# A transformer stack's third feed-forward stage in three packed pairs of steps, with keys and values packed ahead of them

## What is computed

```python
def swiglu(x, w_gu, w_down):
    gate, up = jnp.split(x @ w_gu, 2, axis=-1)
    return (jax.nn.silu(gate) * up) @ w_down

    # first block, layer 0
    x = x + 0.5 * swiglu(rms_norm(x, ffn1_norm[0]), ffn1_w_gu[0], ffn1_w_down[0])      # ffn0
    # gated delta rule and memory attention                                            # ain, mem, out0
    x = x + 0.5 * swiglu(rms_norm(x, ffn2_norm[0]), ffn2_w_gu[0], ffn2_w_down[0])      # ffn1
    ckr = rms_norm(x, kv_in_norm) @ w_dkv
    c_kv = rms_norm(ckr[..., :KV_LORA], kv_lat_norm)
    k_rope = apply_rope(ckr[..., None, KV_LORA:], cos, sin)[:, :, 0]
    k_nope, v_mla = jnp.split((c_kv @ w_ukv).reshape(b, s, B_HEADS, QK_NOPE + V_HEAD), [QK_NOPE], axis=-1)
    # layer 1
    x = x + 0.5 * swiglu(rms_norm(x, ffn1_norm[1]), ffn1_w_gu[1], ffn1_w_down[1])      # ffn2
    # latent attention and memory attention                                            # bin, uq, out1
    x = x + 0.5 * swiglu(rms_norm(x, ffn2_norm[1]), ffn2_w_gu[1], ffn2_w_down[1])      # ffn3
    # second block: pooling, convolutions, differential attention                      # in2, out2
    x = x + (silu(h2 @ w_gate) * (h2 @ w_up)) @ w_down                                 # ffn4
```

## Time and profile before

| | |
|---|---|
| median of three runs | 1291.8 us |
| the profiled execution | 1291.59 us |
| its span | 1289.4 us |
| TensorE (matmuls) busy | 1274.9 us, 99% |
| VectorE busy | 950.1 us, 74% |
| ScalarE busy | 819.0 us, 64% |
| 16 DMA engines moved | 313 MB, 243 GB/s |

### The profile page before, as it was taken

One profiled execution on the slowest core, in us unless ns is written; L12 is line 12 of the kernel. 1 busy time (PEld: TensorE's weight loads), 2 busy tenths in 40 slices (PEclk: granted clock), 3 DMA queues, 4 the chain that ended last, 5 costly groups with the idle time before them and its releaser, 6 DMA issues.

```text
span 1289.4 us, 17186 instructions
## 1 busy us (share of the span) xinstructions
PE 1274.9 (99%) x6940; PEld 1064.7 (83%) x6940; DVE 950.1 (74%) x1105; ACT 819.0 (64%) x1064; POOL 57.2 (4%) x85
## 2 busy tenths in 40 slices
PE   7999999999999999999999999999999999999998
PEld 6888888889988888888787888888888898788887
DVE  5788777778567888776353557678887798688885
ACT  7666658766566666674443466566666857766663
POOL 0000000000000000000000000000000100000000
PEclk9999999999999999999999999999999999999999
DMA  8987748887156677799787766876778874657772
GB/s 338 317 311 226 245 158 287 271 262 228 56 204 249 217 274 263 229 318 312 242 288 249 250 193 189 247 299 228 261 261 258 282 247 154 252 201 259 266 248 70
DMA packets 46686, 313.02 MB, mean 243 GB/s; under 512 B 5196, under 2 KB 7500, under 8 KB 9872
## 3 DMA queue, kind: packets, MB, share of 16 engines
q1 hardware_dynamic: 34080, 227.74, 46.5%
q0 software_dynamic: 11376, 81.54, 25.2%
q10 hardware_dynamic: 1152, 2.66, 0.6%
HBM read 310.85 MB, written 52.44 MB: 282 GB/s over the span
## 4 chain that ended last, share of the span: by engine, by line
PE 94%; DVE 2%; ACT 1%; DMA 1%; issue 0%; SPq 0%; DVEq 0%; ACTq 0%
PE ps L2847 24%; PE ps L2848 24%; PE ps L2849 24%; PE ps L2762 8%; PE ps L2998 2%; PE ps L2773 1%; PE ps L2880 1%; PE ps L2888 1%; PE ps L2893 1%; PE ps L549 1%; PE ps L551 1%; PE ps L550 1%; DVE w_lo_part L1732 1%; DMA arena<-in_tiles 1%; PE ps L2903 1%; PE ps L2820 1%
## 5 line engine op out<-in xcount | busy, mean ns | idle before, releaser
L1732 DVE TENSOR_TENSOR w_lo_part<-w_raw,w_hi_part 128x2048 fp32r<-128x2048 f32 (+2 forms) x184 | 416.2, 2267 | 120.3 <-ACT w_hi_part L674 120.1
L674 ACT ACTIVATE w_hi_part<-w_raw 128x2048 fp32r<-128x2048 f32 (+1 forms) x183 | 346.4, 1896 | 137.3 <-PE ps L2849 129.5
L2847 PE MATMUL ps<-w_hi_part,x_hi 128*128 128x512 f32 (+1 forms) x740 | 289.7, 391 | 0.8 <-DVE w_lo_part L1732 0.5
L2849 PE MATMUL ps<-w_hi_part,x_lo 128*128 128x512 f32 (+1 forms) x740 | 282.4, 382 | 0.0
L2848 PE MATMUL ps<-w_lo_part,x_hi 128*128 128x512 f32 (+1 forms) x740 | 281.4, 380 | 0.0
L2847 PE MATMUL ps<-w_hi_part,h_hi_part 128*128 128x512 f32 x464 | 186.0, 401 | 0.0
L2848 PE MATMUL ps<-w_lo_part,h_hi_part 128*128 128x512 f32 x464 | 181.2, 391 | 0.0
L2849 PE MATMUL ps<-w_hi_part,h_lo_part 128*128 128x512 f32 x464 | 181.2, 391 | 0.0
L674 ACT ACTIVATE w_hi_part<-arena 128x2048 fp32r<-128x2048 f32 x66 | 125.8, 1916 | 68.8 <-DMA arena<-in_tiles 35.9
L1732 DVE TENSOR_TENSOR w_lo_part<-arena,w_hi_part 128x2048 fp32r<-128x2048 f32 x66 | 150.2, 2288 | 24.3 <-ACT w_hi_part L674 23.9
L2849 PEld LDWEIGHTS ps<-w_hi_part,x_lo 128*128 128x128 f32 x740 | 139.1, 188 | 27.5
(11 more groups left out here) (462 smaller groups left out, 1553.4 us busy)
## 6 DMA issues: line engine op xcount, KB each, us to landing
w_raw<-in_tiles SPq DMA_DIRECT2D x179, 1024.0 KB, 6.7
made_sums<-in_tiles POOLq DMA_DIRECT2D x48, 1024.0 KB, 8.3
arena<-made_sums SPq DMA_DIRECT2D x24, 1024.0 KB, 7.8
arena<-in_tiles POOLq DMA_DIRECT2D x18, 1024.0 KB, 11.0
arena<-in_tiles SPq DMA_DIRECT2D x9, 1024.0 KB, 8.5
mem_kv<-in_tiles POOLq DMA_DIRECT2D x6, 1024.0 KB, 10.9
w_raw<-in_tiles SPq DMA_DIRECT2D x3, 512.0 KB, 6.4
arena<-in_w_ukv POOLq DMA_DIRECT2D x1, 1536.0 KB, 14.4
```

Of the source, the lines that this page charges most:

```text
L674: nc.scalar.activation(WH[:, n % RING, 0:w], source(n), ACT.Copy).then_inc(S["w_hi"], 1)
L1732: nc.vector.tensor_tensor(WL[:, n % RING, 0:w], source(n), WH[:, n % RING, 0:w], ALU.subtract).then_inc(S["w_split"], 1)
L2847: nc.tensor.matmul(o, a_hi, w_hi, start=start, stop=False, skip_group_check=True)
L2849: return nc.tensor.matmul(o, a_lo, w_hi, start=False, stop=stop, skip_group_check=True)
```

## The change

ffn2 becomes a stage of packed pairs too, three of them (steps 5, 7, 9). Its steps 0 to 4 stay plain, and all pieces of keys and values stand among them (`late_steps` on TensorE, `from_five` on ScalarE and VectorE). The blocks of x that the sums start from are copied out of PSUM by VectorE there (`x_blocks`), not by ScalarE. Some areas move: the sums' source, one hidden block and the three snapshots of ffn2 lie at the arena's end, the latent and the compressed keys lie further up, the padded rotary keys in the first memory keys' place.

GpSimd's queue makes 30 sums ahead in place of 24, and in another order: three for ffn2 before ffn1, three in ffn2; those for ffn3 from ffn2's third down tile to out1, those for ffn4 one in ffn3 and seven in in2 and out2. SyncE waits for each sum (`made_sum`) and no longer for all of a stage. The load of the two weights of keys and values is issued somewhat sooner. `plain_order`, the plain `ffn` of each engine and the tables of the orders are gone; functions of the stage's name give the orders.

The diff, cut to its core:

```diff
+
+    return (5, 7, 9) if name == "ffn2" else (3, 5, 7, 9)
...
-def quad_order():
-
-    order = [("g0", 0), ("g1", 0), ("g0", 1), ("g1", 1), ("d", 0), ("g0", 2), ("g1", 2)]
-    for s in QUAD_STEPS:
+def quad_order(name):
+
+    first = steps_of(name)[0]
+    order = [("g0", 0), ("g1", 0)]
+    for s in range(1, first):
+        order += [("g0", s), ("g1", s)] + ([("d", s - 1)] if s < first - 1 else [])
+    for s in steps_of(name):
         order += [("p5", s), ("m2", s), ("m1", s), ("p3", s), ("m6", s), ("d", s - 2), ("m7", s), ("d", s - 1), ("m4", s)]
     return order + [("d", 10), ("d", 9)]
...
             def t_load(name, s, k):
 
-                dst, (sem, _) = ((TA[QUAD_STEPS.index(s) % 2], t1_loaded(name, s)), (TC, t3_loaded(name, s)))[k]
+                dst, (sem, _) = ((ta_of(name, s), t1_loaded(name, s)), (TC, t3_loaded(name, s)))[k]
+                sp.wait_ge(*made_sum(name, s, k))
                 sp.dma_start(dst, made[quad_no(name, s), k, :, :]).then_inc(sem, 16)
...
+                if n == unit_of["ffn2", "g1", 4]:
+                    sp.wait_ge(S["kv_ps"], 6)
+                    t_load("ffn2", 5, 0)
+                if n == unit_of["ffn2", "d", 3]:
+                    sp.wait_ge(S["kv_ps"], 11)
+                    t_load("ffn2", 5, 1)
+                    t_load("ffn2", 7, 0)
                 for name in QUADS:
-                    if n == unit_of[name, "g1", 1]:
-                        sp.wait_ge(*made_all(name))
+                    if name != "ffn2" and n == unit_of[name, "g1", 1]:
                         sp.wait_ge(S["x_ready"], 4 * (X_OF[name] - 1) + 1)
-                        t_load(name, QUAD_STEPS[0], 0)
-                    if n == unit_of[name, "d", 0]:
+                        t_load(name, 3, 0)
+                    if name != "ffn2" and n == unit_of[name, "d", 0]:
...
+                def x_blocks(half):
+
+                    for k in range(4):
+                        last = nc.vector.tensor_scalar(blocks[:, 2 * half:2 * half + 2, k, :], PS[:, half:4:2, k * P:(k + 1) * P],
+                                                       gain(name, 4 * half + k), None, ALU.mult)
+                    if half:
+                        last.then_inc(S["x_blocks"], 1)
+
...
+                def from_five():
+
+                    for u in range(4):
+                        turned_hi(name, u)
+                    w_hi(at("g0", 1))
+                    first()
+                    w_hi(at("g1", 1))
+                    gate(0, 0)
+                    gate(0, 1)
+                    act.wait_ge(S["x_blocks"], 2 * of_all(name) + 1)
+                    kv_turned(0)
+                    kv_turned(1)
+                    w_hi(at("d", 0))
+                    hidden_hi(0)
+                    kv_turned(2)
+                    kv_turned(3)
+                    w_hi(at("g0", 2))
+                    gate(1, 0)
+                    gate(1, 1)
+                    w_hi(at("g1", 2))
+                    kv_down(0)
+                    w_hi(at("d", 1))
+                    hidden_hi(1)
+                    kv_down(1)
+                    kv_deviation()
+                    w_hi(at("g0", 3))
+                    sines()
+                    kv_rope()
+                    s_hi()
+                    gate(2, 0)
+                    gate(2, 1)
+                    w_hi(at("g1", 3))
+                    w_hi(at("d", 2))
+                    hidden_hi(2)
...
+                def from_five():
+
+                    start()
+                    w_lo(at("g0", 1))
+                    first()
+                    x_blocks(0)
+                    x_blocks(1)
+                    plain_hidden(0, 0)
+                    plain_hidden(0, 1)
+                    w_lo(at("g1", 1))
+                    hidden_lo(0)
+                    w_lo(at("d", 0))
+                    angles()
+                    w_lo(at("g0", 2))
+                    plain_hidden(1, 0)
+                    plain_hidden(1, 1)
+                    s_sums()
+                    w_lo(at("g1", 2))
+                    lambdas()
+                    w_lo(at("d", 1))
+                    hidden_lo(1)
+                    kv_scaled()
+                    w_lo(at("g0", 3))
+                    plain_hidden(2, 0)
+                    plain_hidden(2, 1)
+                    kv_rope()
+                    w_lo(at("g1", 3))
...
+                    pe.wait_ge(S["x_blocks"], 2 * of_all(name) + 1)
+                    down_half(0, 0)
+                    kv_down(0)
+                    down_half(0, 1)
+                    turn_pair(1)
+                    kv_down(1)
+                    quad_gate_up(2, 0)
+                    kv_turn_rope()
+                    quad_gate_up(2, 1)
+                    kv_swap()
+                    down_half(1, 0)
+                    down_half(1, 1)
+                    turn_pair(2)
+                    kv_turn_latent()
+                    quad_gate_up(3, 0)
+                    kv_keys(0)
+                    quad_gate_up(3, 1)
+                    kv_keys(1)
+                    down_half(2, 0)
+                    kv_keys(2)
+                    down_half(2, 1)
+                    turn_pair(3)
+                    kv_values(0)
+                    quad_gate_up(4, 0, lambda: kv_values(1))
+                    kv_values(2)
+                    quad_gate_up(4, 1)
+                    pe.wait_ge(S["kv_sb"], 14)
+                    for s in steps:
+                        quad_of_steps(s)
+                    down_half(10, 0)
+                    turn_pair(9)
+                    down_half(10, 1)
...
+            def t4_sum(name, s):
+
+                split(name, "m6", s)
+                pool.dma_start(ta_of(name, s), stored(name, "g1", s), accum_op=ALU.add).then_inc(t4_added(name, s)[0], 16)
+
+            def make(name, i):
+
+                copy(name, i)
+                add(name, i)
 
             for s in PAIR_STEPS:
                 pair_sums("ffn0", s)
             paced(tile0["ain"])
             makes("ffn1", 0, [tile0["ain"] + 2 * t + 1 for t in range(6)] + [tile0["mem"], tile0["mem"] + 1])
-            t4_sums("ffn1")
-            pool.wait_ge(S["tile_used"], unit_of["ffn1", "m4", QUAD_STEPS[-1]] + 1)
+            paced(tile0["mem"] + 2)
+            makes("ffn2", 0, [tile0["mem"] + 3])
+            make("ffn2", 1)
+            make("ffn2", 2)
+            for s in steps_of("ffn1"):
+                t4_sum("ffn1", s)
+            pool.wait_ge(S["tile_used"], unit_of["ffn1", "m7", 9] + 1)
             pool.dma_start(KVD, d["w_dkv"].rearrange("p (a b) -> p a b", b=2 * P + ROPE)).then_inc(S["side_loaded"], 16)
+            split("ffn1", "m4", 9)
             pool.dma_start(KVU, d["w_ukv"].rearrange("p (a b) -> p a b", b=2 * BH * P)).then_inc(S["side_loaded"], 16)
-            paced(tile0["ffn2"] + 1)
-            makes("ffn3", 0, range(tile0["ffn2"] + 4, tile0["ffn2"] + 28, 3))
-            paced(tile0["ffn2"] + 27)
-            makes("ffn4", 0, [tile0["ffn2"] + 30])
-            pool.wait_ge(S["kv_ps"], 11)
+            split("ffn2", "g0", 1)
+            makes("ffn2", 3, [unit_of["ffn2", "d", 0], unit_of["ffn2", "g1", 2], unit_of["ffn2", "g0", 3]])
+            makes("ffn3", 0, [unit_of["ffn2", "d", 2], unit_of["ffn2", "g1", 4]])
+            for s in steps_of("ffn2"):
+                t4_sum("ffn2", s)
+            copy("ffn3", 2)
+            split("ffn2", "m4", 9)
             pool.dma_start(RELB[:, :], d["rel_bias"]).then_inc(S["side_loaded"], 16)
             pool.dma_start(TABLE, d["rel_table"]).then_inc(S["side_loaded"], 16)
-            makes("ffn4", 1, [tile0["uq"], tile0["out1"]])
+            add("ffn3", 2)
+            makes("ffn3", 3, [tile0["bin"], tile0["uq"], tile0["uq"] + 1])
             pool.wait_ge(S["bias_row"], 1)
 
             pool.dma_start(bass.AP(bias_line, 0, [[2 * SEQ, MH], [1, 2 * SEQ]]), BROW).then_inc(S["bias_dma"], 16)
             pool.wait_ge(S["bias_dma"], 16)
-            makes("ffn4", 3, [tile0["out1"] + 1, tile0["out1"] + 2])
-            t4_sums("ffn3")
+            makes("ffn3", 6, [tile0["out1"], tile0["out1"] + 1])
+            for s in steps_of("ffn3"):
+                t4_sum("ffn3", s)
+            make("ffn4", 0)
...
+            makes("ffn4", 1, [tile0["in2"] + 2, tile0["in2"] + 4, tile0["in2"] + 6, tile0["in2"] + 8])
+            make("ffn4", 5)
+            make("ffn4", 6)
+            make("ffn4", 7)
+            for s in steps_of("ffn4"):
+                t4_sum("ffn4", s)
```

638 lines of the change are left out of this document (277 added, 361 removed).

## The result

The changed kernel took 1295.9 us (median of 7 runs, 1294.4 to 1298.0), beside it the kernel before 1291.8 us (7 runs, 1290.4 to 1293.6). The ratio is 1.0033, with an interval of 1.0023 to 1.0042: **slower, by 4.1 us** (0.3%, and clear of the noise), where 6.9 us faster was forecast. The profiled execution took 1295.2 us (span 1293.4).

What follows compares the result with a forecast made beforehand. TensorE, busy 99% of the span, was taken to bound the kernel. Terms of -6.9 + 0.2 = -6.7 us on the profiled 1291.6 us gave 1284.9 us, range 1283.4 to 1288.0 us.

Steps and rivals of the forecast that it cites:

- Products: Third feed-forward stage: three packed pairs take out 36 matmuls of 512 columns, 2.31 us a pair, 6.9 us saved.
- Joints: Third stage, tight handovers to TensorE around the moved keys and values: 0.2 us lost for all together.
- (a): VectorE makes eight blocks of x before the second g1 tile's split: 0 us, 1.9 us late at its bound.
- (b): The swap needs ScalarE's rope copy: 1.0 us to spare, so 0 us; 0.5 us late at its bound.
- (c): The latent's turn needs the rotated keys: 0.4 us to spare, so 0 us; up to 1 us late.
- Transfers: GpSimd's six more sums (12 transfers) and SyncE's wait per sum hold up nothing on TensorE: 0 us.
- the second rival: Last stage: GpSimd's in-order chain of sums delays the first pair's accumulating load; slower, 1297 us; chance 0.06.
- The third rival: Third stage: SyncE's queue is stuck in waits, a load comes 5 us late; 1289.9 us, no change; chance 0.05.
- 0 to -0.3 us from the looser waits: Fourth stage: SyncE waiting per sum might save up to 0.3 us; left out of the total.
- A reading of the earlier trace: Claimed TensorE waits once 0.5 us for a weight split, otherwise for such things as 0.2 us for a sum.
- the one on descriptor writing: Skill rule: VectorE in a two-port mode can keep GpSimd from writing descriptors, so added transfers beside out2 could start late.

Runs made afterwards that it cites:

- runs 8: Changed kernel without making the 16 sums of the fourth and fifth feed-forward stages, stored tiles loaded in their place: 1284.35 us, ratio 0.9944.
- 9: Kernel before the change, likewise without making the sums of the fourth and fifth feed-forward stages, stored tiles loaded instead: 1291.5 us, ratio 1.0001.
- 10: Changed kernel with sums begun sooner, unpaced in the third stage, and sum 7 of the last two stages behind an accumulating load: 1288.0 us, ratio 0.9975.
- run 4: Kernel before the change plus an unread spare copy and add of 1 MB each, timed into the last stage's opening: 1295.7 us, ratio 1.0033.
- run 1: Changed kernel with the last stage's sum 7 moved from the opening to behind its first accumulating load: 1291.7 us, ratio 1.0003.
- run 7: Changed kernel with sums spread so that no copy or add is in flight at any opening: 1291.2 us, ratio 1.0000.

## Why the prediction was wrong, point by point

- **Products, -6.9 us: right.** The packed stage by itself was worth 7.2 us in the medians (runs 8 and 9) and 203.4 - 196.6 = 6.8 us in the windows, and the changed kernel without the sums took 1284.35 us where 1284.9 was forecast. Of VectorE, 143.2 us were busy in the stage (146 forecast), and it held nobody up there.
- **Joints (a), (b), (c), 0.2 us: right.** TensorE has no stop before the second g1 tile, the swap or the latent's turn (none at all from 553 to 660 us). In the changed kernel the third stage was idle 0.96 us at one place, the hidden block at 681 us, which no joint covered: ScalarE had waited 6.4 us for the accumulating load of the first pair. Runs 8 and 10 show that the stage can be without it.
- **Transfers, 0 us: this step failed.** The term was put at nothing because the prediction asked only whether each sum is ready in time, and whether GpSimd's queue gets to its accumulating load in time. Both were so: SyncE waited 0.2 us for a sum, the first accumulating load of the last stage went out at 1161.10 us, behind 43.5 us of idle, and the twelve intervals in front of it took 8.6 us each (1014.06 to 1116.78), not 10.3. It did not ask what the transfers do to others that run beside them, though the prediction itself named, under the second rival, that the last ones "run beside the opening of the last stage, when the ring is loaded too". The ring load that stopped TensorE there took 17.5 us instead of 8.5. The price was 11.6 us in all, where the term had 0; in the profiled run 11.4 of it can be placed: the last opening 7.6, the joint 1.9, the fourth stage 0.9, the third stage's first packed pair 1.0.
- **The second rival** had the sign and nearly the time (1297 us), but not the mechanism. The accumulating load was not late by GpSimd's queue; the ring was late by the shared engines. That its time came near is chance. Its chance of 0.06 rested on the intervals of the chain alone.
- **The third rival** did not occur: SyncE waited 5.8 us in the third stage, and behind that neither ScalarE waited for a ring load nor TensorE for anything before the first pair. In the last stage SyncE issued at the same distance from the start as before, and spare transfers in a kernel without the new waits did harm of the same kind (run 4). The new waits were not removed by themselves; what speaks against them is the 0.2 us and run 4.
- **"0 to -0.3 us from the looser waits"**: not seen. The fourth stage was 0.9 us longer, and 174.1 us (174.2 before) where its sums were left out.
- **A reading of the earlier trace rows** was too short: TensorE has longer waits than the 0.5 and 0.2 us named, 5.7 and 1.6 us at the very start of the program. The changed kernel has them too (5.4 and 1.5 us), and they bear on no term.
- The Trainium skill, DMA: Bandwidth & Descriptors, section Rules for kernel authors, says in its row on transfers to disjoint halves that two transfers issued from two engines share the same DMA engines, their packets interleaved. The trace agrees: beside the add queue 1 has 33.1% of the engines, alone 100.3%, and the load took 17.5 us for 8.5. It was the rule to weigh in the prediction, in the place of the one on descriptor writing, of which no run here shows anything.

Still open: how the lateness is spread over the places in an ordinary run. Each kernel has one profile, and the runs of one kernel differ by up to 12 us where the kernel before differs by 3.

## What to carry to other kernels

A background transfer is not free because its result is early: look at what else is in flight when it runs, and count the room in each stretch by the DMA share (0.62 and 0.63 in the stretches that took more sums; 0.78 and 0.87 after) and by the loads that have a due time there. (That the share decides is a reading of these stages; only the place of the transfers was varied, not the share by itself.) A stage that was slow on the compute engine may have been where such transfers hid; when it is packed, its transfers must go somewhere, so their place belongs to the sum. When the median moves, compare the spread too: of the kernels with late loads most spread over 4 to 12 us (the changed kernel itself over 3.6, run 4 over 2.9), those without over 2 to 3.5, and in run 1 that told of a cause which one good profile hid.

## What the runs showed of the hardware that was not expected

- An add from memory to memory costs the engines about twice the time per byte of a load beside it: 67.8% for 0.93 MB against 33.1% for 0.88 MB (above); the full engines then move 274 GB/s, not 420. The copy costs no more than a load (0.70 MB in 47.0% against 0.79 MB in 54.5%, 426 GB/s in all).
- A stop of TensorE is not paid by its length alone. Behind the 4.40 us stop the granted clock was 0.50 for 5.6 us (the lower level), and behind the 1.99 us stop of run 10 for 3.2 us; behind the 2.37 us stop of run 7 it stayed at 1.00. The windows of the three, in that order:

```profile
1136.10:1141.70 5.60, 5.58 (x15) 4.55 (x16) 5.50 (x7) 3.42 (x3) 0.00 (x0) 0.50 0.55 190
```
```profile
1134.40:1137.60 3.20, 3.20 (x10) 2.45 (x9) 3.13 (x4) 1.73 (x2) 0.00 (x0) 0.50 0.73 294
```
```profile
704.70:712.00 7.30, 7.23 (x32) 5.96 (x33) 5.88 (x7) 3.45 (x3) 0.83 (x1) 1.00 1.00 422
```

So the length of a stop alone does not tell whether the clock falls; why it did not in the last case is not settled by these runs.
